# Two picks at once on TensorE's column halves, and twelve front pieces in the lead-in, in a decoder trunk with expert retrieval

## The reference

```python
best_s, best_pos = lax.top_k(cand.reshape(tb, PEER_HEADS, kk * kk), kk)
expert = jnp.take_along_axis(cand_idx.reshape(tb, PEER_HEADS, kk * kk), best_pos, axis=-1)
gate = jax.nn.softmax(best_s, axis=-1)
u = u_tab[expert]
act = jax.nn.gelu(jnp.einsum('td,thkd->thk', xb, u), approximate=False)
w = (gate * act).astype(xb.dtype)
return jnp.einsum('thk,thkd->td', w, v_tab[expert])
```

## Time and profile before

| | |
|---|---|
| median of three runs | 3395.55 us |
| profiled execution, its span | 3410.71 us, 3408.9 us |
| granted TensorE clock, mean | 0.916 |
| busy: TensorE, VectorE, ScalarE, GpSimd | 2680.2, 2298.1, 733.0, 2010.4 us |
| read from HBM | 1181.52 MB, 347 GB/s over the span |
| V matmuls (L1305), 3520 instructions | 1794.8 us busy |
| V weight loads (L1305), 3520, mean of one | 203 ns |
| U products (L1032), 1024 | 1250.3 us busy |
| V adds on VectorE (L1042), 144 | 185.0 us busy |

### The profile page before, as it was taken

One profiled execution on the slowest core, in us unless ns is written; L12 is line 12 of the kernel. 1 busy time (PEld: TensorE's weight loads), 2 busy tenths in 40 slices (PEclk: granted clock), 3 DMA queues, 4 the chain that ended last, 5 costly groups with the idle time before them and its releaser, 6 DMA issues.

```text
span 3408.9 us, 26586 instructions
## 1 busy us (share of the span) xinstructions
PE 2680.2 (79%) x7136; PEld 1259.5 (37%) x7136; DVE 2298.1 (67%) x4976; ACT 733.0 (22%) x1629; POOL 2010.4 (59%) x2074
## 2 busy tenths in 40 slices
PE   7784578789898777888988777878998776666768
PEld 3454133344454332334444333334454322222223
DVE  1559966786578876777588876777478874455542
ACT  2321211232221121223222121223222111111111
POOL 0012576655566666666665667755666666666665
PEclk9796789889999899889999898889999999989889
DMA  5135899988999999998999999998999999999998
GB/s 184 72 140 193 281 381 407 407 325 327 387 392 371 368 358 407 407 377 325 395 406 371 361 365 408 406 376 296 384 407 385 343 358 369 374 356 383 375 355 327
DMA packets 351448, 1185.46 MB, mean 348 GB/s; under 512 B 37666, under 2 KB 38212, under 8 KB 351044
## 3 DMA queue, kind: packets, MB, share of 16 engines
q0 software_dynamic: 294912, 1073.87, 82.8%
q1 hardware_dynamic: 56388, 109.88, 8.7%
HBM read 1181.52 MB, written 2.10 MB: 347 GB/s over the span
## 4 chain that ended last, share of the span: by engine, by line
PE 26%; DVE 22%; issue 17%; POOL 17%; DMA 14%; another core or an unknown queue 4%; ACT 1%; DVEq 0%; POOLq 0%
PE peer_acc L1305 14%; DMA v_ring<-in_peer_v,experts 9%; POOL v_ring L513 9%; POOL u_ring L513 8%; DVE u_ring L1032 6%; DMA u_ring<-in_peer_u,experts 4%; PE act_bank L1091 3%; PE dve_bank L1091 2%; DVE work L798 2%; DVE work L787 1%; PE act_bank L1192 1%; DVE work L795 1%; DVE work L784 1%; DVE work L979 1%
## 5 line engine op out<-in xcount | busy, mean ns | idle before, releaser
L1305 PE MATMUL peer_acc<-v_ring,diag 128*128 128x512 f32 x3520 | 1794.8, 648 | 536.3 <-DMA v_ring<-in_peer_v,experts 411.0
L1032 DVE SCALAR_TENSOR_TENSOR u_ring<-u_ring,h_now 128x1024 f32<-128x1024 f32 x1024 | 1250.3, 1221 | 711.3 <-DMA u_ring<-in_peer_u,experts 546.8
L513 POOL DMA_INDIRECT u_ring<-in_peer_u,experts x1024 | 995.9, 973 | 725.7 <-issue 288.7
L513 POOL DMA_INDIRECT v_ring<-in_peer_v,experts x1024 | 1009.0, 985 | 658.1 <-PE peer_acc L1305 297.7
L1305 PEld LDWEIGHTS peer_acc<-v_ring,diag 128*128 128x128 f32 x3520 | 670.5, 203 | 1538.9 <-issue 757.0
L715 ACT ACTIVATE diag<-ident,wts 128x128 f32<-128x128 f32 x880 | 326.8, 396 | 1483.3 <-PE peer_acc L1305 794.1
L1091 PE MATMUL act_bank<-w_ring,hT 128*128 128x512 f32 x768 | 361.7, 619 | 8.8 <-ACT decay L682 4.2
L1042 DVE SCALAR_TENSOR_TENSOR xs<-v_ring,wts,xs 128x1024 f32<-128x1024 f32 x144 | 185.0, 1285 | 73.6 <-DMA v_ring<-in_peer_v,experts 62.4
L1091 PEld LDWEIGHTS act_bank<-w_ring,hT 128*128 128x128 f32 x768 | 155.7, 204 | 213.7 <-issue 208.9
L1178 PE MATMUL act_bank<-hT,w_ring 128*128 128x256 f32 x768 | 178.0, 388 | 31.5 <-ACT mix L555 31.5
L1178 PEld LDWEIGHTS act_bank<-hT,w_ring 128*128 128x128 f32 x768 | 149.5, 195 | 67.2 <-issue 47.7
(11 more groups left out here) (159 smaller groups left out, 1587.3 us busy)
## 6 DMA issues: line engine op xcount, KB each, us to landing
w_ring<-in_w_in SPq DMA_DIRECT2D x24, 2048.0 KB
w_ring<-in_peer_w_q SPq DMA_DIRECT2D x16, 2048.0 KB
w_ring<-in_w_out SPq DMA_DIRECT2D x8, 2048.0 KB
u_ring<-in_peer_u,experts POOLq DMA_INDIRECT x1024
v_ring<-in_peer_v,experts POOLq DMA_INDIRECT x1024
xs<-in_x SPq DMA_DIRECT2D x4, 512.0 KB, 7.5
keysT<-in_peer_sub_keys SPq DMA_DIRECT2D x2, 1024.0 KB
out<-xs SPq DMA_DIRECT2D x4, 512.0 KB
```

Of the source, the lines that this page charges most:

```text
L513: pool.indirect_dma_start(ring[:, n % depth, :], None, table, bass.IndirectOffsetOnAxis(ap=experts[:, tile % TILES, e:e + 1], axis=0),).th ...
L1032: tell(nc.vector.scalar_tensor_tensor(out=row, in0=row, scalar=1.0, in1=h_now[:], op0=ALU.mult, op1=ALU.mult, accum_out=dots[:, c % 2, s:s ...
L1305: ins = nc.tensor.matmul(peer_acc[:, j * 512:(j + 1) * 512], diag[:, (v_count(c, s) - 1) % DIAGS, :], v_ring[:, n % V_RING, j * 512:(j + 1 ...
```

## The change

**V for two picks.** A chunk's 16 picks are paired: pick q with pick q + 8. The V gather of an even slot loads, in partitions 0 to 63, pick q of tokens 0 to 63 and, in partitions 64 to 127, pick q + 8 of the same 64 tokens; the odd slot does so for tokens 64 to 127. For that the indices and the weights are laid out anew (`pair_experts`, `pair_wts`): VectorE writes the halves that stay in their partitions (two small instructions beside the old one, at each of 32 routings and 64 chunks), and two small DMAs issued by ScalarE carry the halves that cross (64 rows of 2 x 32 bytes at a routing, 64 rows of 32 bytes at a chunk). The stationary operand is `ident2`, the 64 x 64 identity twice, scaled: 128 rows by 64 columns. The even slot's product goes to output partitions 0 to 63, the odd slot's to 64 to 127, in turn for each 512 columns.

**All V on TensorE.** `vector_slot` and the adds on VectorE are gone; 1024 slots are 512 pairs. `v_used` is one semaphore for each half, `diag` holds six pairs, ScalarE makes it eight slots ahead, Gelu and the product with the gates stand two slots earlier, the move of the weights one slot after the product. A chunk's first V gather of a routing also waits for `experts_moved`.

**The lead-in.** 12 pieces stand in slots -32 to -1; the 16 others of the 28 are spread over slots 0 to 127 on top of what stands there. The table `due_at` is the same from slot 128 on.

```diff
-DIAGS = 10
+DIAGS = 6
-V_EVERY = 8
+SIDE = P // 2
+FIRST_LEAD = 12
-D_AHEAD = 7
-GELU_BEFORE = D_AHEAD + 4
-WTS_BEFORE = D_AHEAD + 2
+D_AHEAD = 8
+GELU_BEFORE = D_AHEAD + 5
+WTS_BEFORE = D_AHEAD + 3
+MOVE_BEFORE = D_AHEAD + 2
...
+        FIRST_LOAD = sum(loads[PARTS_ALONE:PARTS_ALONE + FIRST_LEAD])
...
-            goal = min((n + U_AHEAD) * LEAD_LOAD // U_AHEAD, LEAD_LOAD)
+            goal = min((n + U_AHEAD + 1) * FIRST_LOAD // U_AHEAD, FIRST_LOAD)
+            goal += min(max(n + 1, 0), PH * SLOTS) * (LEAD_LOAD - FIRST_LOAD) // (PH * SLOTS)
             goal += max(n + 1, 0) * FRONT_LOAD // (HALF * PH * SLOTS)
...
+                c, s = divmod(n, SLOTS)
+                if s == 0 and c % HPC == 0:
+                    pool.wait_ge(experts_moved, 32 * (call_of(c) + 1))
                 if n >= V_RING:
-                    old_c, old_s = divmod(n - V_RING, SLOTS)
-                    pool.wait_ge(v_added if by_vector(old_c, old_s) else v_used, v_count(old_c, old_s))
-                gather(v_rows, v_ring, V_RING, v_landed, *divmod(n, SLOTS))
+                    pool.wait_ge(v_used[n % 2], (n - V_RING) // 2 + 1)
+                gather(v_rows, v_ring, V_RING, v_landed, pair_experts, n, c % PH * TOPK + s % 2 * FEW + s // 2)
...
+                    if part == 4:
+                        call = k * QJ * HALF + n
+                        act.wait_ge(routed, call + 1)
+                        if call:
+                            act.wait_ge(experts_moved, 32 * call)
+                        to, of = split(pair_experts[:, t0 + i, :]), split(experts[:, t0 + i, :])
+                        act.dma_start(to[SIDE:P, heads, 0, :], of[0:SIDE, heads, 1, :]).then_inc(experts_moved, 16)
+                        act.dma_start(to[0:SIDE, heads, 1, :], of[SIDE:P, heads, 0, :]).then_inc(experts_moved, 16)
...
+            def move(c):
+                act.wait_ge(wts_ready, c + 1)
+                to, of = pair_wts[:, c % 2, :], wts[:, c % 2, :]
+                act.dma_start(to[SIDE:P, 0:FEW], of[0:SIDE, FEW:SLOTS]).then_inc(wts_moved, 16)
+                act.dma_start(to[0:SIDE, FEW:SLOTS], of[SIDE:P, 0:FEW]).then_inc(wts_moved, 16)
...
+                if q == 0:
+                    act.wait_ge(wts_moved, 32 * (c + 1))
+                n = c * FEW + q
+                for side in range(2):
+                    if n >= DIAGS:
+                        act.wait_ge(v_used[side], n - DIAGS + 1)
+                    ins = nc.scalar.activation(diag[:, n % DIAGS, side * SIDE:(side + 1) * SIDE], ident2[:], ACT.Copy,
+                                               scale=pair_wts[:, c % 2, side * FEW + q:side * FEW + q + 1])
+                ins.then_inc(diag_ready, 1)
...
+                for side in range(2):
+                    m = 2 * n + side
+                    pe.wait_ge(v_landed[m % V_RING], 16 * (m // V_RING + 1))
+                pe.wait_ge(diag_ready, n + 1)
                 for j in range(D // 512):
+                    for side in range(2):
+                        rows = slice(side * SIDE, (side + 1) * SIDE)
+                        ins = nc.tensor.matmul(peer_acc[rows, j * 512:(j + 1) * 512], diag[:, n % DIAGS, rows],
+                                               v_ring[:, (2 * n + side) % V_RING, j * 512:(j + 1) * 512],
+                                               start=(pair == 0), stop=(pair == PH * FEW - 1))
+                        if j == D // 512 - 1:
+                            ins.then_inc(v_used[side], 1)
```

111 lines of the change are left out of this document (48 added, 63 removed).

## The result

The changed kernel takes 3412.85 us (median of 9 runs, 3402.63 to 3424.48), the kernel before, in the same session, 3390.71 (9 runs, 3383.72 to 3400.23). The ratio is 1.0064, interval 1.0044 to 1.0084: slower by some 22 us (0.64%), where 3350 us was forecast and 3405 was the upper end of the stated range.

The account below looks back on a forecast made before the run. The prediction took the kernel as bound by the DMA row stream, 407 GB/s at best, with time to regain only where it is thin. Terms -34 - 36 - 7 + 8 + 5 + 8 + 10 = -46 us gave 3350 us, range 3288 to 3405.

Parts of the forecast that it names:

- Rings in twos, +10: V buffers come back in twos and TensorE's clock is low more often: +10 us (0 to 40) for both.
- The middles, -36: Three middles of a front, where TensorE returns `v_ring` late: halved V work gives 3 x -12 us, between 0 and -94.
- The start, -34: Shorter lead-in: 40 us sooner at slot 43, 6 given back by slot 127; -34 us, between -55 and 0.
- ScalarE, +8: Emptying of PSUM banks queued behind ScalarE's wait in the middles: about 12 chunks at 0.7 us, +8 (0 to 54).
- slower through ScalarE: Rival: waits for moved weights in the middles and routings in route stretches, 96 places, 1.5 us each; 3486 us, chance 0.12.
- The drain, -7: Last 31 V gathers, issued over 46 us behind TensorE, take 39 us: -7 us, between 0 and -7.
- VectorE's +8: Two more small instructions at 32 routings and 64 chunks, counting only where VectorE is full: +8 us (0 to 34).
- the DMA's +5: 16384 rows of 32 bytes more on the same DMA engines: +5 us, 0 to 86.
- the pairing by count: Gathers paired with the buffer's use six before: buffers explain none of 61.7 us idle in 2800 to 3340; that stretch stays.
- more comes back: Rival: V matmuls do hold the last stretch, so its 49.2 us of waits go too; 3300 us, chance 0.12.
- the halves run in turn: Rival: the array's halves don't run side by side, a pair costs 3.44 us; 3423 us, chance 0.07.
- The start gives nothing: Rival: deferred route pieces in slots 0 to 127 cost more than the lead-in saved; 3384 us, chance 0.12.

Follow-up runs that it names:

- lead12_only: The kernel before with the new order of front pieces (lead-in of twelve pieces) alone, V as before; ratio 0.9916 to the kernel before.
- own_late: The changed kernel with the edits of own_slot and late_moves together; ratio 0.9907 to the kernel before.
- late_moves: The changed kernel, but ScalarE waits for a routing and moves its picks one routing later; ratio 1.0007 to the kernel before.
- own_slot: The changed kernel, but each slot's two 64-column matmuls stand at their own slot with own landing wait and release; ratio 0.9957 to the kernel before.
- v7u5: late_moves with seven V and five U buffers instead of six and six; ratio 0.9890 to the kernel before.
- no_moves: The changed kernel without transfers between partition halves and without ScalarE's waits for them, half the picks and weights being other rows'; ratio 1.0005 to the kernel before.
- the mixed kernel: own_late, but with pairs at the odd slot wherever an output, mid or query piece is due, 146 of 512; ratio 0.9953 to the kernel before.
- filler: The changed kernel with two more matmuls of a zero tile into the low half of `peer_acc` at each even slot; ratio 1.0085 to the kernel before.

## Why the prediction was wrong

The sum of the prediction can be laid beside one of ratios. With 3390.7 us as 1: lead-in -28 (lead12_only), V in single slots on halves against the old V -3 with 13 to each side (own_late against lead12_only), pairs with their common release +34 (late_moves against own_late), ScalarE's waits for routings +19 (late_moves against after). Together +22, the measured difference. It closes by construction; the terms are what counts, and each has some 8 to 13 us of error. Beside the forecast's own terms, as an estimate: of the 68 us between -46 and +22 the middles' gain that didn't come is 34, the rings are some 23, ScalarE 11, the drain 10 and the start 6, and some 16 come back because VectorE's and the DMA's terms were put too high.

**Rings in twos, +10: some +33.** The prediction put "+10 (0 to 40) for both" rings and clock, because at full pace the earlier buffer comes back 2.6 us later and "TensorE keeps up even then". Pairs with their common release cost 34 us, with the middles and the drain in it. TensorE did keep up. The ring did not: it was judged by TensorE's rate and not by how long a buffer is held. In slots 50 to 127 a V buffer is held for 16.6 us in own_slot, over six buffers 2.8 us a slot, and for 17.2 in this kernel, 2.9; the stream at its best gives a slot in 2.57. An estimate from these means says only that six buffers were short already. What the longer hold does is in the waits by count: in slots 32 to 127 GpSimd waits for V buffers for 21 us before, 29 in own_slot, 49 in this kernel and 6 in v7u5. v7u5 gets back 1.2%, some 40 us, at the same low clock, so the ring accounts for the whole term and the clock isn't needed for it. The prediction said rightly that nothing on TensorE can shorten a stretch at 407 GB/s, and never asked whether something can lengthen it.

**The middles, -36: nothing came, the largest miss.** 320, 337, 336 GB/s after, windows above 350 had been named. The V gathers of the same slots (128 to 178, 384 to 434, 640 to 690) take 162, 155 and 162 us before and 164, 155 and 159 after, 2 us less in all. TensorE's time was not what held them. In 680 to 840 it is busy for 21 us less and idle for 21 us more, and its waits there name VectorE, before for 10.4 us in all, now for 29.0. The longest, first of before, then of after:

```profile
PE dve_bank L1273 <- DVE a_intra L922: 6.4, 1, 6.4
```

```profile
PE dve_bank L1291 <- DVE a_intra L941: 6.4, 1, 6.4
PE dve_bank L1283 <- DVE work L891: 5.3, 1, 5.3
PE dve_bank L1241 <- DVE work L891: 5.2, 2, 4.3
PE act_bank L1093 <- DVE mix L983: 3.7, 1, 3.7
```

These are products of the front that wait for VectorE's steps, and the V matmuls stand behind them in TensorE's order. The prediction had the reason in hand as its bound "the ends are 0 (VectorE decides)" and took 8 to 12 us a middle from a busy share of 95%. That VectorE would decide with V buffers to spare as well is likely from v7u5, where the wait moves to U products, but not shown, since its U ring is shorter too. The row "GpSimd waits 44.4 us for V matmuls" was right about the buffer and said nothing of why those matmuls were late.

**The start, -34: -28.** The first V gather came at 318.73, not near 309, since the first U gather was 4.8 us later (it lies between 234 and 243 us in the kernels above) and the lead-in 5 us longer. V number 43 came at 452.1 against 484.8, 33 us sooner where 35 were forecast. In lead12_only, where nothing else is changed, the V gathers are 42 us ahead at slot 32, as forecast (40), but 27 at slot 128, where 34 were to be left. Of what the lead-in gains, then, 16 us are given back by slot 128 and not 6.

**ScalarE, +8: +19, and in another place.** The prediction had 12 chunks at 0.7 us for the waits for moved weights. Those can't be seen: no_moves and late_moves are level, with 8 us to each side. The cost is at a wait that it named for the route stretches alone, and gave no term in the sum. Every front's last routing ends where the next front's first norm begins, and the new wait stands ahead of that norm. The rival *slower through ScalarE* had the right engine, and one of its two waits; its price, 0.55 to 1.5 us at each of 96 places, was wrong, since the starts of the fronts made most of it: there the V gathers of this kernel fall behind late_moves', by 4 us from slot 32 to 64, by 3 from 256 to 288 and by 6 from 512 to 544, 13 of the 17 us by which the two part after slot 0.

**The drain, -7: +3.** The last 31 V gathers took 49.3 us (3351.3 to 3400.6), before 46.3. The timeline of this kernel there:

```profile
3390.02 0.94 POOL L504 DMA_INDIRECT v_ring<-in_peer_v,pair_experts  x1 [0.64 <-PE peer_acc L1324]
3391.26 0.94 POOL L504 DMA_INDIRECT v_ring<-in_peer_v,pair_experts  x1 [0.30 <-issue]
3391.27 1.94 PE L1324 MATMUL peer_acc<-v_ring,diag 128*64 128x512 f32 x8 [1.49 <-issue]
3393.44 0.94 POOL L504 DMA_INDIRECT v_ring<-in_peer_v,pair_experts  x1 [1.24 <-PE peer_acc L1324]
3394.64 1.94 PE L1324 MATMUL peer_acc<-v_ring,diag 128*64 128x512 f32 x8 [1.43 <-issue]
3394.69 0.94 POOL L504 DMA_INDIRECT v_ring<-in_peer_v,pair_experts  x1 [0.30 <-issue]
...
3399.99 1.94 PE L1324 MATMUL peer_acc<-v_ring,diag 128*64 128x512 f32 x8 [0.89 <-issue]
```

TensorE idles before each pair, and GpSimd waits for the first buffer of every pair. The gathers at 3393.44 and 3394.69 are for the pair at 3399.99: 5.3 us from the second issue to the start, 1.9 for the pair. Three pairs go round in such a turn, and GpSimd waits for one of them to end. This stretch before was paced by TensorE without a pause, and now it is paced by the ring.

**VectorE's +8 and the DMA's +5.** The small transfers have a queue of their own on the page:

```profile
q10 hardware_dynamic: 19456, 0.54, 0.3%
```

0.3% of the engines' span are some 10 us, near the 6 forecast, and no_moves, which hasn't got them, is level with late_moves: their price in time is 0 within 8 us. VectorE's small instructions can't be told apart from V's move to the halves; together they are the -3, so they were either small or paid for by what TensorE and VectorE save.

**What held.** The halves run side by side: 1.94 us for eight instructions, at the forecast's "near 1.9". By the Trainium skill's sentence (TensorE: Matmul & The Clock Gate, Part 3) that weight loads overlap only where `row_grp` differs, the pair would have cost near 1.6 us more; the trace does not agree. The last stretch stayed at 369 GB/s with 83 us less of work on TensorE in it (382 and 299), so the pairing by count was right and the page's "49.2 us for V matmuls" was not; this kernel's row for it is no smaller, and in v7u5, with a seventh V buffer, the same stops have another name:

```profile
POOL v_ring L504 <- PE peer_acc L1324: 52.7, 17, 4.5
```

```profile
POOL v_ring L504 <- remote: 61.5, 19, 4.6
...
POOL v_ring L504 <- PE peer_acc L1331: 8.9, 13, 2.8
```

The rivals *more comes back* and *the halves run in turn* are out. *The start gives nothing* is out by lead12_only.

What stays open: what GpSimd's idle time is that no ring explains; why the mixed kernel loses where it does, outside the middles; and what the low clock by itself costs the pairs.

## What to carry to other kernels

Before merging two uses of a ring into one, compare how long a buffer is held with the ring's depth times the pace: merging holds the first of the two longer (14.7 us here, against 12.1 when each slot stands alone), and where the stream is at its limit this costs even if the engine does the work in half the time. When a wait is put on an engine's queue, look at what stands behind it at the seams between stages, not at how many waits there are; here the one at each front's first norm cost most of it, and standing one routing later cost nothing. Before relieving an engine that the profile names as late, ask what that engine itself waits for: here TensorE was late with V because its other work waited for VectorE. And try one buffer more first, since that alone shows the next wait's name.

## What the runs showed of the hardware

With the packed and pausing work TensorE's granted clock was lower, 0.825 over the span where it had been 0.916, and 0.71 in the window 2800 to 3360, where its work is 299 of 560 us; the filler, 984 us busy in the profile, brought it back to 0.941. The time did not follow it: two forms at 0.826 and 0.923 take 3358.9 and 3359.1 us, and filler has 1.0085 where this kernel has 1.0064, no faster. What the lower clock costs by itself no run separates from what the lighter work gives. Two halves of 64 columns with all rows in use take 1.94 us for eight instructions of 512 columns in single precision, and 1.90 us for four of them on one half alone (own_late), so the second half is nearly free at that clock:

```profile
2902.72 1.90 PE L1328 MATMUL peer_acc<-v_ring,diag 128*64 128x512 f32 x4 [1.53 <-DMA v_ring<-in_peer_v,pair_experts]
```

GpSimd's idle time without a cause in either ring lasts through all seventeen kernels (231 to 314 us), with TensorE busy for 2267 to 2851 us in them.
